# GpSimd's gated norm in quarter pieces, a merge tile that starts before its last input third, and a last output tile in two column groups

## The reference, cut to what matters

```python
o_g = o_gla * lax.rsqrt(jnp.mean(o_gla * o_gla, axis=-1, keepdims=True) + NORM_EPS)
o_g = (o_g.astype(x.dtype) * gla_g).reshape(B, T, GLA_VAL_WIDTH) * jax.nn.silu(z_b)
mix = jax.nn.sigmoid(g_a) * (o_nsa @ w_ba) + jax.nn.sigmoid(g_b) * (o_g @ w_bb)
return x + mix @ w_out          # then y = rms_norm(x + ..., final_norm_g)
```

## Time and profile before

| | us |
|---|---|
| median of 3 runs | 1355.89 (1353.88 to 1356.62) |
| span of the profiled execution | 1354.8 |
| PE busy in it | 1298.8 (96%) |
| DVE, ACT, POOL busy | 619.4, 621.8, 145.7 |

### The profile page before, as it was taken

One profiled execution on the slowest core, in us unless ns is written; L12 is line 12 of the kernel. 1 busy time (PEld: TensorE's weight loads), 2 busy tenths in 40 slices (PEclk: granted clock), 3 DMA queues, 4 the chain that ended last, 5 costly groups with the idle time before them and its releaser, 6 DMA issues.

```text
span 1354.8 us, 23612 instructions
## 1 busy us (share of the span) xinstructions
PE 1298.8 (96%) x9533; PEld 1170.1 (86%) x9533; DVE 619.4 (46%) x1387; ACT 621.8 (46%) x1072; POOL 145.7 (11%) x184
## 2 busy tenths in 40 slices
PE   5999998999999999999999999999988989999998
PEld 4999998999988889989888889888866779999876
DVE  6211145645834343433323333466578767453342
ACT  6211336542555536666556645665467542221121
POOL 2100001103300000000000300313010260000000
PEclk9999999999999999999999999999999999899999
DMA  7251453522422211122212221554345656452331
GB/s 207 63 171 42 120 149 103 147 69 61 79 69 59 64 59 60 48 79 64 65 59 79 60 59 52 172 168 147 101 155 197 245 180 193 136 157 64 109 121 59
DMA packets 156908, 145.27 MB, mean 107 GB/s; under 512 B 27360, under 2 KB 141360, under 8 KB 156736
## 3 DMA queue, kind: packets, MB, share of 16 engines
q1 hardware_dynamic: 154016, 135.33, 33.1%
q0 software_dynamic: 2784, 8.43, 2.1%
HBM read 105.88 MB, written 41.88 MB: 109 GB/s over the span
## 4 chain that ended last, share of the span: by engine, by line
PE 56%; ACT 2%; DVE 2%; issue 1%; SPq 0%; DMA 0%; another core or an unknown queue 0%; POOL 0%; DVEq 0%; ACTq 0%
PE ps L240 31%; PE ps L2536 7%; PE ps L1645 4%; PE ps L1679 4%; PE ps L1661 3%; PE ps L1694 1%; PE ps L2443 1%; PE ps L2411 1%; DVE S L2648 1%; PE ps L2447 1%; PE ps L1764 1%; PE ps L2544 1%; PE ps L2502 0%; DMA m_raw<-in_w_branch_a 0%; SPq L3012 0%
## 5 line engine op out<-in xcount | busy, mean ns | idle before, releaser
L240 PE MATMUL ps<-hH,wH 128*128 128x352 f32 (+1 forms) x1320 | 440.0, 333 | 5.8 <-DVE stg L375 3.0
L240 PE MATMUL ps<-hH,wL 128*128 128x352 f32 (+1 forms) x1320 | 425.3, 322 | 0.0
L240 PE MATMUL ps<-hL,wH 128*128 128x352 f32 (+1 forms) x1320 | 424.8, 322 | 0.0
L240 PEld LDWEIGHTS ps<-hH,wH 128*128 128x128 f32 (+1 forms) x1320 | 248.1, 188 | 32.9 <-issue 26.5
L240 PEld LDWEIGHTS ps<-hL,wH 128*128 128x128 f32 (+1 forms) x1320 | 249.1, 189 | 2.2 <-issue 1.9
L240 PEld LDWEIGHTS ps<-hH,wL 128*128 128x128 f32 (+1 forms) x1320 | 247.8, 188 | 0.3
L227 DVE TENSOR_TENSOR wL<-w_raw,wH 128x1024 fp32r<-128x1024 f32 (+1 forms) x70 | 87.8, 1254 | 132.8 <-ACT wH L219 132.7
L2002 DVE CUSTOM_DVE_ANT_0 sP<-ps,dist,stat 128x256 f32<-128x256 f32 (+3 forms) x116 | 58.6, 542 | 176.8 <-issue 108.2
L360 ACT ACTIVATE stg<-ps 128x352 f32<-128x352 f32 x132 | 61.1, 463 | 119.1 <-PE ps L240 117.3
L219 ACT ACTIVATE wH<-w_raw 128x1024 fp32r<-128x1024 f32 (+1 forms) x70 | 73.5, 1050 | 70.5 <-issue 39.5
L2199 ACT ACTIVATE pPT<-ps 128x512 f32<-128x512 f32 x74 | 44.1, 596 | 131.9 <-PE ps L1661 131.8
(11 more groups left out here) (391 smaller groups left out, 2035.1 us busy)
## 6 DMA issues: line engine op xcount, KB each, us to landing
w_raw<-in_w_in SPq DMA_DIRECT2D x61, 512.0 KB, 4.1
p_spill<-stg SPq DMA_DIRECT2D x132, 176.0 KB, 1.8
zt<-p_spill SPq DMA_DIRECT2D x24, 528.0 KB, 4.8
w_raw<-in_w_in SPq DMA_DIRECT2D x17, 256.0 KB, 3.8
gvT<-p_spill SPq DMA_DIRECT2D x8, 528.0 KB, 5.4
x_all<-in_x_prompt SPq DMA_DIRECT2D x8, 512.0 KB, 10.0
m_raw<-in_w_branch_b SPq DMA_DIRECT2D x8, 512.0 KB, 5.5
xr<-in_x_prompt SPq DMA_DIRECT2D x8, 512.0 KB, 3.5
```

Source lines behind the costliest of these rows:

```text
L240: mm = nc.tensor.matmul(ps[0:t.m, bank, 0:NF], w[:, c % 2, t.m * k:t.m * k + t.m], x[n][:, k, :], start=(k == 0 and i == 0), stop=(k == t. ...
```

## The change

Three parts. (1) `normed` runs four instructions of two token tiles each per head in place of one, and `og_normed` counts each; turns 0 and 1 of a block wait for what they read (two pieces and four pieces of the head), the turn of the sample rows only for the sample rows. (2) Tile 8 runs its first seven blocks of k in all three banks after seven rests, then waits for the eighth and runs the last block; the wait for all eight ahead of the loop is gone. (3) The last output tile's second half is done as two groups of 256 columns in different banks, 24 matmuls each. The first group's add, square, variance part and weight multiplication are DVE and ACT work of its own, the first half of 512 gets its weight early and is scaled at the end by ACT, and SP stores columns 512 to 1023 first and then 0 to 511.

```diff
@@ def turn(p):
-                pe.wait_ge(sem("og_normed"), f // 2 + 1)
                 if j == 2:
                     pe.wait_ge(sem("sample_normed"), f // 2 + 1)
+                else:
+                    pe.wait_ge(sem("og_normed"), 4 * (f // 2) + 2 * j + 2)
@@ def tile(c):
+                if c == KT:
+                    pe.wait_ge(sem("og_low"), KT - 1)
+                    for n in range(3):
+                        mring.products(c, n, 3 * (c % 2) + n, xH, xL, 0, KT - 1)
+                    pe.wait_ge(sem("og_low"), KT)
+                    for n in range(3):
+                        mm = mring.products(c, n, 3 * (c % 2) + n, xH, xL, KT - 1, KT)
+                    mm.then_inc(sem("m_f_done"), 1)
+                    return
...
-            pe.wait_ge(sem("og_low"), KT)
             for c in range(KT, 2 * KT):
                 tile(c)
@@ def out_products(t, half, bank, ks, cols=slice(0, 512)):
-                        mm = nc.tensor.matmul(ps[0:n, bank, :], m, w[half][:, k, :],
+                        mm = nc.tensor.matmul(ps[0:n, bank, cols], m, w[half][:, k, cols],
@@ last output tile on PE
                     mm.then_inc(sem("y_half"), 1)
+                    out_products(t, 1, pairs[n % 4][1], range(KT), slice(0, 256)).then_inc(sem("y_half"), 1)
+                    pe.wait_ge(sem("y_added"), n - 2)
+                    out_products(t, 1, pairs[(n + 1) % 4][1], range(KT), slice(256, 512)).then_inc(sem("y_done"), 1)
+                    continue
@@ def normed(h):
-                nc.gpsimd.tensor_tensor(ogv[:, 0:PT, h, :], ogv[:, 0:PT, h, :],
-                                        grv[:, 0:PT, h].unsqueeze(2).to_broadcast([P, PT, DV]), ALU.mult)\
-                    .then_inc(sem("og_normed"), 1)
+                for t in range(0, PT, 2):
+                    nc.gpsimd.tensor_tensor(ogv[:, t:t + 2, h, :], ogv[:, t:t + 2, h, :],
+                                            grv[:, t:t + 2, h].unsqueeze(2).to_broadcast([P, 2, DV]), ALU.mult)\
+                        .then_inc(sem("og_normed"), 1)
@@ def y_add(n), last tile
+                nc.vector.tensor_tensor(y[:, 0:512], y[:, 0:512], fg[:, 0:512], ALU.mult).then_inc(sem("half_var"), 1)
+                dve.wait_ge(sem("y_half"), 2)
+                nc.vector.tensor_tensor(y[:, 512:768], ps[:, b + 1, 0:256], x[:, 512:768], ALU.add)\
+                    .then_inc(sem("y_added"), 1)
+                dve.wait_ge(sem("y_squared"), n + 2)
+                dve.wait_ge(sem("half_var"), 1)
+                nc.vector.scalar_tensor_tensor(out=fst[:, 22:23], in0=fst[:, 21:22], scalar=1.0 / D, in1=fst[:, 20:21],
+                                               op0=ALU.mult, op1=ALU.add).then_inc(sem("half_var"), 1)
+                link(nc.vector.tensor_tensor(y[:, 512:768], y[:, 512:768], fg[:, 512:768], ALU.mult))
                 dve.wait_ge(sem("y_done"), n + 1)
-                nc.vector.tensor_tensor(y[:, 512:D], ps[:, b + 1, :], x[:, 512:D], ALU.add).then_inc(sem("y_added"), 1)
+                nc.vector.tensor_tensor(y[:, 768:D], ps[:, pairs[(n + 1) % 4][1], 256:512], x[:, 768:D], ALU.add)\
+                    .then_inc(sem("y_added"), 1)
@@ def y_finish(n), last tile
+                nc.vector.reciprocal(r, ss).then_inc(sem("y_var"), 1)
+                dve.wait_ge(sem("y_var"), n + 2)
+                nc.vector.tensor_scalar(y[:, 512:768], y[:, 512:768], r, None, ALU.mult).then_inc(sem("y_ready"), 1)
+                nc.vector.scalar_tensor_tensor(out=y[:, 768:D], in0=y[:, 768:D], scalar=r, in1=fg[:, 768:D],
+                                               op0=ALU.mult, op1=ALU.mult).then_inc(sem("y_ready"), 1)
@@ ACT, last tile
-                    y_square(yy[:, n % 3, 512:D], ss, n + 2)
+                    y_square(yy[:, n % 3, 512:768], fst[:, 21:22], n + 2)
+                    y_square(yy[:, n % 3, 768:D], ss, n + 3)
...
+            act.wait_ge(sem("half_var"), 2)
+            act.wait_ge(sem("y_var"), TILES + 1)
+            half = yy[:, (TILES - 1) % 3, 0:512]
+            nc.scalar.activation(half, half, ACT.Copy, scale=fst[:, 2 * TILES - 1:2 * TILES]).then_inc(sem("y_sd"), 1)
@@ SP, last tile
+                sp.wait_ge(sem("y_ready"), n + 2)
+                sp.dma_start(dst[:, 512:D], yy[:, n % 3, 512:D]).then_inc(sem(f"y_stored{n % 3}"), 16)
+                sp.wait_ge(sem("y_sd"), TILES + 1)
+                sp.dma_start(dst[:, 0:512], yy[:, n % 3, 0:512]).then_inc(sem(f"y_stored{n % 3}"), 16)
```

More of the change, by code:

```diff
@@ L2526, in _, with out_products @@
                 tile(c)
-            pe.wait_ge(sem("og_low"), KT)
             for c in range(KT, 2 * KT):
                 tile(c)
-            def out_products(t, half, bank, ks):
+            def out_products(t, half, bank, ks, cols=slice(0, 512)):
                 n = rows_of(t)
@@ L2826, in y_finish @@
                 else:
-                    dve.wait_ge(sem("y_squared"), n + 2)
-                    dve.wait_ge(sem("half_var"), 1)
-                    nc.vector.scalar_tensor_tensor(out=r, in0=ss, scalar=1.0 / D, in1=fst[:, 20:21], op0=ALU.mult,
+                    dve.wait_ge(sem("y_squared"), n + 3)
+                    dve.wait_ge(sem("half_var"), 3)
+                    nc.vector.scalar_tensor_tensor(out=r, in0=ss, scalar=1.0 / D, in1=fst[:, 22:23], op0=ALU.mult,
                                                    op1=ALU.add).then_inc(sem("y_var"), 1)
                 dve.wait_ge(sem("y_sd"), n + 1)
[L2832 to L2836, removed]
-                                                   op1=ALU.mult).then_inc(sem("y_ready"), 1)
+                y = yy[0:m, n % 3, :]
+                if n < TILES - 1:
+                    link(nc.vector.reciprocal(r, ss))
+                    nc.vector.scalar_tensor_tensor(out=y, in0=y, scalar=r, in1=fg[0:m, :], op0=ALU.mult,
+                                                   op1=ALU.mult).then_inc(sem("y_ready"), 1)
+                    return
+                nc.vector.reciprocal(r, ss).then_inc(sem("y_var"), 1)
[3 more added lines that the diff above has]
+                                               op0=ALU.mult, op1=ALU.mult).then_inc(sem("y_ready"), 1)
             for n in range(TILES):
@@ L3077, in _ @@
                     load_x(n + 3)
-                sp.wait_ge(sem("y_ready"), n + 1)
                 dst = y_p[0, P * t:P * t + P, :] if t < PT else y_s.rearrange("b s d -> (b s) d")
[L3080 to L3084, removed]
+                if n < TILES - 1:
+                    sp.wait_ge(sem("y_ready"), n + 1)
+                    sp.dma_start(dst, yy[0:rows_of(t), n % 3, :]).then_inc(sem(f"y_stored{n % 3}"), 16)
+                    continue
+                sp.wait_ge(sem("y_ready"), n + 2)
+                sp.dma_start(dst[:, 512:D], yy[:, n % 3, 512:D]).then_inc(sem(f"y_stored{n % 3}"), 16)
+                sp.wait_ge(sem("y_sd"), TILES + 1)
+                sp.dma_start(dst[:, 0:512], yy[:, n % 3, 0:512]).then_inc(sem(f"y_stored{n % 3}"), 16)
             for s, count in enumerate((3, 3, 4)):
```

## The result

The changed kernel takes 1346.87 us (median of 6 runs, 1346.0 to 1348.73), the kernel before 1354.89 us in the same comparison (6 runs, 1350.56 to 1356.62). The ratio is 0.9936, 95% interval 0.992 to 0.9952: 0.6% less, about 8 us, as forecast (1347.9 us, -0.59%). The change is small beside the spread of single executions (6 us in the kernel before), so what follows is read from distances within traces first and from run times second.

What follows compares the result with a forecast made beforehand. TensorE waits of 3.29 us at turn 2 and 2.7 us before tile 8 were taken as bounds: -2.5 - 2.7 - 2.9 + 0.1 = -8.0 us, span 1346.8, with 1.1 around it 1347.9 us; range 1346.3 to 1349.3, with two rivals to 1351.3.

Steps and rivals of the forecast that it cites:

- who gets the operands when GpSimd's instructions stand in a row: Norm beside tile 2's weight rest: DVE gets in between two GpSimd instructions, so it waits 0 to 1.06 us.
- the 1.1 us around the span: Time outside the profiled span: 1.1 us, from the span of 1354.8 us against a median of 1355.89 us.
- the +0.5 us for the split last tile: Last output tile: 48 matmuls of 256 columns for 24 of 512 cost +0.5 us, between +0 and +0.8.
- the low clock at tile 8: Tile 8: removing PE's idle time keeps the clock up, saving 2.9 us, bounds 0 to 3.0.
- The first wait: PE's 3.29 us idle ahead of turn 2, behind tile 2's weight rest: quarter pieces save 2.5 us, 1.6 to 3.0.
- The mean wait for a piece: Tile 2's weight rest on DVE waits 0.5 us in the mean for the GpSimd piece in flight.
- the rival in which GpSimd keeps the operands: DVE's rest would wait for all sixteen norm pieces; 1355.9 us at 1.06 us a piece, 1361 at 1.41; chance 0.04.
- Late next: Block 0's rest and tile 3's weight rest may wait 1.0 us together; 1.7 us of slack before turn 5 covers it.
- Tile 8: PE's wait for the last rest goes, saving 2.7 us, and the low clock behind it, saving 2.9 us.
- a rival whether the clock would fall after the change: Clock still falls after another short idle time, or tile 8's fall had another cause; 1350.8 us, chance 0.14.
- The other half: Steps behind the last matmul, with smaller add and square and a sooner second store: -0.4 to -0.5 us.

Runs made afterwards that it cites:

- e5_held: Changed kernel with norm heads 0 to 2 whole and the last head's pieces held until tile 2's weight rest is done; 1346.78 us, ratio 0.9943.
- e7_eighths: Changed kernel with eight norm pieces of 128x256 per head, 32 in all, in place of quarters; 1353.81 us in one run.
- e4_fill: Kernel before with 16 unused matmuls put ahead of tile 8's wait, which stays; 1354.29 us, ratio 0.9992.
- e10_fill1: Kernel before with quarter pieces and 16 unused matmuls ahead of tile 8's wait, which stays; 1350.38 us, ratio 0.9958.
- e1_part1: Kernel before with only the norm in quarter pieces and its waits; 1351.75 us, ratio 0.9981.
- e3_part3: Kernel before with only the last output tile's change; 1353.0 us, ratio 0.9978.

## Why the forecast time came out, and which steps of the prediction failed

The time was forecast at 1347.9 us and measured at 1346.87, and the saving within the span at 8.0 us and, by distances, measured at 8.0. Parts 1 and 2 rest on mechanisms that the experiments bear out. The step that failed is the answer to who gets the operands when GpSimd's instructions stand in a row: from one edge the prediction concluded that DVE gets in between any two, and with pieces of 0.57 us it waited 7.1 us, to the end of the norm. Three terms were mis-sized besides: the 1.1 us around the span (2.1 measured in the changed kernel), the +0.5 us for the split last tile (0.13), and the low clock at tile 8, taken as a fixed 2.9 us (2.63 in one execution, 1.5 and 1.4 in two others). That the time came out in spite of them is in part luck: the changed kernel's span was 1344.7 us, 2.1 less than the forecast 1346.8, nearly all of it from stages ahead of the change, and what lies around the span was 1.0 us more.

- **The first wait.** The mechanism was right: DVE's two-input rest waited for the GpSimd instruction in flight, which `e5_held` shows by taking it away. The saving was 2.3 us for a forecast 2.5 (by the prediction's own times, idle from 1105.99 to 1106.7 in place of 3.29 us, it would be 2.6). The mean wait for a piece was set at 0.5 us. It was 0.6 to 0.8 us in all five profiled executions with quarter pieces: the rest comes due at much the same phase of GpSimd's row each time. Piece edges are 1.00 us apart, not 1.06.
- **The argument about edges failed.** From one edge between two instructions of 2.33 us I concluded that DVE gets in between any two, and gave the rival in which GpSimd keeps the operands 0.04, with the danger in pieces longer than 1.1 us. For the change's 1.00 us the conclusion held. The rival is real, though, and lies on the other side: with pieces of 0.57 us DVE waited to the end of the norm, twice. The step took the result for all lengths, and it took it from the wrong kind of instruction: L2655 in the earlier trace rows is a TENSOR_SCALAR with one input tile. In `e7_eighths` such an instruction (L2669) still got in at an edge, and the two-input rest did not. The row could not tell the two apart. (The rival's own time was off as well: 16 pieces of 1.06 us end at 1110.2, not 1110.6.)
- **Late next.** The slack of 1.7 us ahead of turn 5 held: the rest of block 0 took 1.57 us and not 1.26, and turn 5 came 7.03 us after turn 2, as before.
- **Tile 8.** Forecast 2.7 + 2.9, measured 2.76 + 2.63, parted by the distance that `e4_fill` has with the wait and without the fall. The clock term was 0.3 us too large because it compared a tile after a pause with one in a run: at full clock the former takes 12.0 us from the last rest to the take-over (`e10_fill1`) and the latter 11.6. The fall's length varies: in `e1_part1` the low clock cost 1.53 us (60.74 - 59.21), in `e3_part3` 1.4 (62.13 us from turn 2 to take-over, less 59.21 and less the 1.57 lost behind turn 2).
- **The clock was taken for a fixed cost.** Its size and, at turn 2, its coming vary: the fall at tile 8 cost from 1.4 to 2.6 us in three profiles, one at turn 2 came in one profile of four, and 33 of 48 executions of the kernel before ran at a mean clock of 0.994 or less. The text weighed in a rival whether the clock would fall after the change, but not that it already rises and falls from run to run in the kernel before, at turn 2 as well. The profiled execution, at a mean clock of 0.995, was not typical: 0.993 was the most frequent value in the timed ones. By the first group's run times the low clock costs the median execution some 3.9 us (1355.22 - 1351.3, an estimate, and it holds falls elsewhere too), more than the term of 2.9.
- **The last tile.** The split was set at +0.5 us and cost 0.13. The row of 256-column matmuls that I leaned on reads strided columns (0.132 us apart); these stand at 0.119, near the floor of 0.116 that half a 512-wide one gives. The Trainium skill's rule in "TensorE: Matmul & The Clock Gate", section "Back-to-back issue gap", gave +0.05, an estimate, nearer than my choice. The other half was off by the same amount: the span ends 0.46 us sooner as forecast (-0.45), but the device time behind the last matmul only 0.07. The two errors cancel.
- **Around the span.** 1.1 us was the wrong number. It set one execution's span against other executions' median. Each run's own time is 1.7 to 1.8 us above its span with the old last tile and 2.0 to 2.2 with the new one, so the profiled execution of before had taken some 1356.5 us, an estimate.

## What to carry to other kernels

An idle time of TensorE costs itself and can cost clock behind it: here the wait of 2.7 us brought 1.4 to 2.6 us more in each of three profiles, one of 3.3 us in one of four. One profile doesn't show such a cost; look at several executions. Before such a wait is attacked elsewhere, ask which of the waiting product's operands are already there: 21 of tile 8's 24 groups of three matmuls needed nothing that was late. When GpSimd and VectorE both work from SBUF, look at what GpSimd has in flight at the moment a critical two-input VectorE instruction is due. Shorter pieces help, but only down to a length: at 0.57 us a piece TensorE stood 7.2 us at turn 2, and 3.3 with whole heads, while holding back the work that isn't urgent (`e5_held`) left 0.2.

## What was not expected of the hardware

- A queue of GpSimd instructions of 0.57 us from one to the next kept a DVE instruction with two SBUF inputs out for 7.1 us, while one of 1.00 us let it in at the first edge. The Trainium skill, "SBUF — State Buffer", section "Who interferes with whom", says that whoever issues first gets the shared ports for the whole instruction while the other blocks. The traces agree for instructions of 1.00, 2.33 (there with a single-input DVE instruction) and 3.6 us and do not for 0.57: there the block outlasts the instruction and ends with the queue.
- Single-input DVE instructions wait too: L2669 on 32x4 elements took 0.99 us beside quarter pieces in the changed kernel and 0.14 beside whole heads in `e3_part3` (L2659 there), where an edge fell at that moment. What follows it on ScalarE still ended before it was needed.
- The device time around the span rose from about 1.75 to 2.1 us with the new last tile, and to 2.2 or 2.3 with 32 GpSimd pieces as well. What it depends on stays open.
- Code that is the same in all kernels here differs by up to 5.3 us in where it stands at 1090 us, and the number of earlier falls of the clock goes with it. Against that, changes of under 1 us can only be read as distances within a trace.
